# Two transformer blocks: the first norm's factor moves from the input of the first two loads to their drains, and the first load comes in two halves

## The reference, cut to what matters

```
def rms_norm(x, g):
    y = x * rsqrt(mean(x * x, axis=-1, keepdims=True) + EPS)
    return y * g

h = rms_norm(x, norm_mix_g)
proj = h @ w_in                              # [256, 7 * 1024]
sc_b, sc_c, sc_x, cf_a, cf_g, gate_sc, gate_cf = split(proj)
cf = (cf_a + cf_b_pw1[:1024]) * sigmoid(cf_g + cf_b_pw1[1024:])
```

## Time and profile before

| | |
|---|---|
| median of three executions | 1431.58 us (1431.01 to 1433.02) |
| profiled execution, its time | 1430.79 us |
| its span (first to last instruction) | 1428.7 us |
| TensorE busy | 1309.6 us, 92% |
| DVE, ACT, POOL busy | 945.6, 498.5, 452.0 us |
| mean granted clock of TensorE | 0.971 |
| first matmul of the first load | 11.55 us |
| first matmul of a split load | 27.40 us |

### The profile page before, as it was taken

One profiled execution on the slowest core, in us unless ns is written; L12 is line 12 of the kernel. 1 busy time (PEld: TensorE's weight loads), 2 busy tenths in 40 slices (PEclk: granted clock), 3 DMA queues, 4 the chain that ended last, 5 costly groups with the idle time before them and its releaser, 6 DMA issues.

```text
span 1428.7 us, 25109 instructions
## 1 busy us (share of the span) xinstructions
PE 1309.6 (92%) x9622; PEld 1233.8 (86%) x9622; DVE 945.6 (66%) x2085; ACT 498.5 (35%) x973; POOL 452.0 (32%) x326
## 2 busy tenths in 40 slices
PE   9999999999999987886888787888899999999998
PEld 8999999998888986886878786878886789989997
DVE  4689987675594775859586767755525546666665
ACT  5533456445223121211202221211225445553443
POOL 1588822000133654453635453564203000000000
PEclk9999999999999999898989999999999999999999
DMA  7555554552599999999999999999862023465552
GB/s 280 195 190 189 178 177 165 190 177 92 215 424 353 419 426 428 427 428 427 428 426 426 427 425 428 426 428 427 352 255 83 29 90 133 149 203 181 177 185 81
DMA packets 57895, 397.91 MB, mean 279 GB/s; under 512 B 6352, under 2 KB 9040, under 8 KB 10192
## 3 DMA queue, kind: packets, MB, share of 16 engines
q0 software_dynamic: 36864, 268.45, 44.9%
q1 hardware_dynamic: 20944, 128.28, 25.3%
HBM read 395.66 MB, written 1.05 MB: 278 GB/s over the span
## 4 chain that ended last, share of the span: by engine, by line
PE 57%; DMA 20%; DVE 12%; issue 6%; ACT 3%; POOL 1%; DVEq 0%; POOLq 0%; ACTq 0%
DMA rows_late<-peer_uv_dram,stage 20%; PE bank L765 11%; PE bank L767 11%; PE bank L766 11%; PE bank L1023 7%; PE bank L728 6%; PE bank L749 4%; DVE rows_late L2105 4%; ACT w_hi L1259 1%; PE bank L889 1%; POOL rows_late L665 1%; DVE probs L2029 1%; DVE probs L2031 1%; DVE pick L2032 1%; DVE w_lo L548 1%
## 5 line engine op out<-in xcount | busy, mean ns | idle before, releaser
L1023 PE MATMUL bank<-diag,rows_late 128*128 128x128 f32 x2816 | 325.1, 277 | 26.3 <-ACT diag L1452 26.3
L1023 PEld LDWEIGHTS bank<-diag,rows_late 128*128 128x128 f32 x2816 | 321.3, 194 | 29.2 <-ACT diag L1452 29.1
L2105 DVE SCALAR_TENSOR_TENSOR rows_late<-rows_late,squares 128x1024 f32<-128x1024 f32 x176 | 213.1, 1228 | 127.1 <-DMA rows_late<-peer_uv_dram,stage 111.0
L1023 PE MATMUL bank<-diag,rows_early 128*128 128x128 f32 x1280 | 172.7, 302 | 75.4 <-ACT diag L1452 75.4
L1023 PEld LDWEIGHTS bank<-diag,rows_early 128*128 128x128 f32 x1280 | 167.2, 215 | 81.4 <-ACT diag L1452 80.9
L665 POOL DMA_INDIRECT rows_late<-peer_uv_dram,stage x165 | 192.8, 1169 | 136.9 <-PE bank L1023 95.0
L1259 ACT ACTIVATE w_hi<-raw 128x2048 fp32r<-128x2048 f32 x94 | 179.3, 1909 | 118.2 <-PE bank L767 109.9
L765 PE MATMUL bank<-x_hi_a,w_hi 128*128 128x256 f32 x672 | 190.9, 284 | 2.7 <-DVE x_lo_a L1672 1.8
L766 PE MATMUL bank<-x_lo_a,w_hi 128*128 128x256 f32 x672 | 190.2, 283 | 0.0
L767 PE MATMUL bank<-x_hi_a,w_lo 128*128 128x256 f32 x672 | 190.1, 283 | 0.0
L548 DVE TENSOR_TENSOR w_lo<-raw,w_hi 128x2048 fp32r<-128x2048 f32 x66 | 151.2, 2292 | 49.9 <-ACT w_hi L1259 45.2
(11 more groups left out here) (357 smaller groups left out, 1877.3 us busy)
## 6 DMA issues: line engine op xcount, KB each, us to landing
raw<-w_in_dram SPq DMA_DIRECT2D x28, 1024.0 KB, 5.0
raw<-w_up_dram SPq DMA_DIRECT2D x16, 1024.0 KB, 5.0
raw<-w_down_dram SPq DMA_DIRECT2D x16, 1024.0 KB, 4.9
rows_late<-w_in_dram SPq DMA_DIRECT2D x10, 1024.0 KB, 8.5
raw<-w_kv_dram SPq DMA_DIRECT2D x8, 1024.0 KB, 4.8
rows_late<-w_peer_q_dram SPq DMA_DIRECT2D x5, 1024.0 KB, 12.2
raw<-sc_w_out_dram SPq DMA_DIRECT2D x4, 1024.0 KB, 4.8
raw<-cf_w_pw_dram SPq DMA_DIRECT2D x4, 1024.0 KB, 4.8
```

The lines of the kernel that those rows point to most:

```text
L1023: mm = nc.tensor.matmul(ct(Y_ACC[c][t // 4], t % 4, P), expert_rows(k)[:, D + t * P:D + (t + 1) * P], ct(diag, k % DIAGS, P), start=False, ...
L2105: w_.scalar_tensor_tensor(out=row, in0=row, scalar=1.0, in1=h_tok[:, c * D:(c + 1) * D], op0=ALU.mult, op1=ALU.mult, accum_out=pre[:, side ...
```

## The change

Before its matmuls of the first two loads TensorE no longer waits for the norm's factor. DVE multiplies x by the norm's weights alone into a free buffer (gate_cf) as soon as vec and x are there, and the plain matmuls read that. The factor is the same for a whole column of an output tile, so it enters at the drains. The statistics run behind the fifth input tile of load 0, the spread behind the seventh; the fillers between them are gone, and two more stand in the opening. DVE copies the spread factor to SBUF (rstd), makes h_norm from gate_cf and rstd for the later loads, and drains g0 and g1 to SBUF times rstd; ACT's sigmoid then works in place there. For a0 and a1 DVE first multiplies the bank by rstd into a small buffer (turns) and then does the former instruction on that. ACT's rounding of load 2 now stands in front of its roundings of h. SP issues load 0 in two halves right behind vec, ahead of the identity, and load 2 ahead of the other constants.

```
--- before.py
+++ after.py
@@ -98,7 +98,7 @@
         p.append((None, 0, [(name, first + i) for i in range(n)], engine))
 
     for b in range(4):
-        add("w_in", [16 + b], "g", 2, "act", 2 * b)
+        add("w_in", [16 + b], "g", 2, "act" if b else "dve", 2 * b)
         add("w_in", [12 + b], "a", 2, "dve", 2 * b)
     for b in range(4):
         add("w_in", [4 + b], "c", 2, "act", 2 * b)
@@ -594,11 +597,13 @@
                 sp.dma_start(whole(i), T[name][b]).then_inc(whole_landed[at], 16)
 
             sp.dma_start(vec[:], T["vecs"]).then_inc(vec_landed, 16)
+            name, b = LOADS[0]
+            sp.dma_start(ring(raw, 0)[:, 0:SLOT // 2], T[name][b][:, 0:SLOT // 2]).then_inc(first_half_landed, 16)
+            sp.dma_start(ring(raw, 0)[:, SLOT // 2:], T[name][b][:, SLOT // 2:]).then_inc(raw_landed[0], 16)
             sp.dma_start(ident, T["consts"][:, 0:P]).then_inc(ident_landed, 16)
-            load(0)
             load(1)
+            load(2)
             sp.dma_start(const[:, P:], T["consts"][:, P:]).then_inc(const_landed, 16)
-            load(2)
             sp.dma_start(mem_raw.rearrange("p (t s) -> p t s", t=DT),
                          T["mem_t"].rearrange("(t p) s -> p t s", p=P)).then_inc(mem_landed, 16)
             sp.dma_start(pos_i, T["positions_2"].to_broadcast([P, SEQ])).then_inc(pos_landed, 16)
@@ -737,16 +742,22 @@
                     pe.wait_ge(query_landed[n - RING], 16)
                 else:
                     w = ring(raw, i)
-                    pe.wait_ge(raw_landed[i % RING], 16 * RAW_COUNT[i])
+                    if i:
+                        pe.wait_ge(raw_landed[i % RING], 16 * RAW_COUNT[i])
+                    else:
+                        pe.wait_ge(first_half_landed, 16)
                 outs = [open_tile(name, n) for n in which]
+                x_gain = h_norm if norm_name == "peer" else gate_cf
                 for k in range(DT):
+                    if i == 0 and k == DT // 2:
+                        pe.wait_ge(raw_landed[0], 16)
                     if norm_name == "peer":
                         pe.wait_ge(peer_scaled, k + 1)
                     else:
-                        pe.wait_ge(normed, NORMED[norm_name] - DT + k + 1)
+                        pe.wait_ge(x_gained, k + 1)
                     for j, out in enumerate(outs):
                         at = k * 256 + j * P
-                        mm = nc.tensor.matmul(out[:, 0:SEQ], w[:, at:at + P], ct(h_norm, k),
+                        mm = nc.tensor.matmul(out[:, 0:SEQ], w[:, at:at + P], ct(x_gain, k),
                                               start=(k == 0), stop=(k == DT - 1))
                         if k == DT - 1:
                             mm.then_inc(acc_ready, 1)
@@ -915,22 +926,26 @@
                                  start=False, stop=True).then_inc(acc_ready, 1)
 
             pe.wait_ge(filled, 2)
-            keep_busy(10)
+            keep_busy(12)
             pe.wait_ge(filled, 4)
-            for j in range(DT // 2):
-                pe.wait_ge(summed, j + 1)
-                for c in range(NC):
-                    mm = nc.tensor.matmul(STAT[:, c:c + 1], ct(squares, 2 * j)[:, c * P:(c + 1) * P], mean_d[:, 0:1],
-                                          start=(j == c == 0), stop=(j == DT // 2 - 1 and c == NC - 1))
-                if j == DT // 2 - 1:
+
+            def first_norm(k):
+
+                if k == 4:
+                    for j in range(DT // 2):
+                        pe.wait_ge(summed, j + 1)
+                        for c in range(NC):
+                            mm = nc.tensor.matmul(STAT[:, c:c + 1], ct(squares, 2 * j)[:, c * P:(c + 1) * P],
+                                                  mean_d[:, 0:1], start=(j == c == 0),
+                                                  stop=(j == DT // 2 - 1 and c == NC - 1))
                     mm.then_inc(stat_ready, 1)
-                keep_busy(1 if j < DT // 2 - 1 else 2)
-            pe.wait_ge(ident_landed, 16)
-            spread("mix")
-            keep_busy(1)
+                elif k == 6:
+                    pe.wait_ge(ident_landed, 16)
+                    spread("mix")
+
             for b in range(4):
                 if b == 0:
-                    linear_plain("g", range(2), LOAD_OF["g", 0], "mix")
+                    linear_plain("g", range(2), LOAD_OF["g", 0], "mix", first_norm)
                     linear_plain("a", range(2), LOAD_OF["a", 0], "mix")
                 else:
                     linear("g", range(2 * b, 2 * b + 2), "w_in", 16 + b, "h1", DT, 256)
@@ -1340,10 +1355,16 @@
             square("mix", lambda k: act.wait_ge(x_landed[k // 4], 16), x_res)
             act.wait_ge(filled, 6)
             root("mix")
+            round_to(2)
             split_all("h1", normed_tile("mix"), h_norm)
             for b in range(4):
                 for i in range(2 * b, 2 * b + 2):
-                    drain("g", i, ct(sig, i), ACT.Sigmoid, bias=v("cf_b_pw1", 8 + i))
+                    if b:
+                        drain("g", i, ct(sig, i), ACT.Sigmoid, bias=v("cf_b_pw1", 8 + i))
+                    else:
+                        ahead("g", i)
+                        wait_drained(act, "g", i)
+                        s.activation(ct(sig, i), ct(sig, i), ACT.Sigmoid, bias=v("cf_b_pw1", 8 + i)).then_inc(first_sig, 1)
                 ahead("a", 2 * b)
                 if b == 0:
                     act.wait_ge(mem_landed, 16)
@@ -1697,21 +1718,40 @@
             def freed(ins):
                 return done(ins, acc_freed["dve"])
 
-            for j in range(DT // 2):
-                dve.wait_ge(squared, square_count("mix", 2 * j + 1))
-                w_.tensor_tensor(ct(squares, 2 * j), ct(squares, 2 * j), ct(squares, 2 * j + 1), ALU.add).then_inc(summed, 1)
             dve.wait_ge(vec_landed, 16)
-            norm("mix", x_res, "norm_mix_g", h_norm)
+            for half in range(2):
+                dve.wait_ge(x_landed[half], 16)
+                for k in range(4 * half, 4 * half + 4):
+                    w_.tensor_scalar(ct(gate_cf, k), ct(x_res, k), v("norm_mix_g", k), None, ALU.mult).then_inc(x_gained, 1)
+                for j in range(2 * half, 2 * half + 2):
+                    dve.wait_ge(squared, square_count("mix", 2 * j + 1))
+                    w_.tensor_tensor(ct(squares, 2 * j), ct(squares, 2 * j), ct(squares, 2 * j + 1), ALU.add).then_inc(summed, 1)
+            dve.wait_ge(x_gained, DT)
+            link(w_.tensor_copy(rstd[:], rstd_of("mix")))
+            for k in range(DT):
+                tok = done(w_.tensor_tensor(ct(h_norm, k), ct(gate_cf, k), rstd[:], ALU.mult), normed)
+            dve.wait_ge(*tok)
             split_all("h1", h_norm)
+            for i in range(2):
+                wait_tile(dve, "g", i)
+                freed(w_.tensor_tensor(ct(sig, i), acc("g", i), rstd[:], ALU.mult))
 
             dve.wait_ge(filled, 4)
             for i in range(8):
                 ahead("a", i)
                 wait_tile(dve, "a", i)
-                wait_drained(dve, "g", i)
-                tok = freed(w_.scalar_tensor_tensor(out=ct(cf_in, i, CFW)[:, CFK - 1:], in0=acc("a", i),
-                                                    scalar=v("cf_b_pw1", i), in1=ct(sig, i),
-                                                    op0=ALU.add, op1=ALU.mult))
+                if i < 2:
+                    dve.wait_ge(*freed(w_.tensor_tensor(turns[:], acc("a", i), rstd[:], ALU.mult)))
+                    dve.wait_ge(first_sig, i + 1)
+                    tok = done(w_.scalar_tensor_tensor(out=ct(cf_in, i, CFW)[:, CFK - 1:], in0=turns[:],
+                                                       scalar=v("cf_b_pw1", i), in1=ct(sig, i),
+                                                       op0=ALU.add, op1=ALU.mult), dve_step)
+                    dve.wait_ge(*tok)
+                else:
+                    wait_drained(dve, "g", i)
+                    tok = freed(w_.scalar_tensor_tensor(out=ct(cf_in, i, CFW)[:, CFK - 1:], in0=acc("a", i),
+                                                        scalar=v("cf_b_pw1", i), in1=ct(sig, i),
+                                                        op0=ALU.add, op1=ALU.mult))
                 if i == 1:
                     for k in range(DT):
                         add_to_sum("mem", k)
```

More of the change, by code:

```diff
@@ L447, in two_blocks @@
         vec_landed = sem("vec_landed")
+        first_half_landed = sem("first_half_landed")
+        x_gained = sem("x_gained")
+        first_sig = sem("first_sig")
         ident_landed = sem("ident_landed")
```

## The result

The changed kernel took 1438.99 us (median of 6 runs, 1437.93 to 1440.37) against 1432.12 for the kernel before (6 runs, 1431.01 to 1433.63): ratio 1.0047, 95% interval 1.0037 to 1.0057. That is 6.9 us slower, where 0.9 us faster was forecast. So the two profiles are 9.6 us apart where the medians are 6.9 apart.

A forecast was written before the change was run, and what follows sets the result against it. TensorE, busy for 92% of the span, was taken as the bound. Split matmuls 1.1 us earlier plus 0.2 us of new wait gave -0.9 us, from 1431.58 to 1430.7 us; range 1428.8 to 1432.6.

The forecast's parts named there:

- The start: Opening: load matmuls wait only for the first gained tile and half load, so start at 8.3, 3.25 us earlier.
- Statistics and spread among the matmuls: Opening on TensorE: statistics groups add about 1.7 us, the spread 0.5; root and reciprocal are hidden behind tiles 5 and 6.
- The clock in the opening: Under the load matmuls: 1.2 GHz from 9.1 to 12.6, costing 1.75 us; first split matmul at 26.3, 1.1 us earlier.
- The drains: DVE's chain after the spread: products 2.77 us, mem sums 3.59, w_lo of load 4 ready at 38.25; g's banks cause no wait.
- The wait for w_lo of load 4: TensorE before load 4's split matmuls: wants w_lo at 38.24, waits between 0 and 0.9 us, taken as 0.2.
- so it moves along: Later stretch bound by the expert rows' DMA: begins when TensorE's scores are known, so it shifts with TensorE; no term given.
- a gain at 50 us is not there any more at the end: Sign of being wrong: a lead won in the opening has vanished by the kernel's end.
- R3: DVE's chain takes over: the wait for w_lo of load 4 is 0.9 to 1.1 us, total 1431.5; chance 0.12.
- R1: Opening: the clock doesn't fall, split matmuls start from 24.6, total 1429.0 us; chance 0.17.
- R2: Opening: the clock falls and stays low as long as before, costing 3.4 us, total 1432.2; chance 0.16.
- R4: Opening: the half load lands no sooner than the whole (9.6), total 1432.3 us; chance 0.05.
- The range: Total time from 1428.8 to 1432.6 us, reaching from R1 to R2 with half a microsecond of scatter.

The follow-up runs named there:

- f1_probe: The kernel before with one more POOL subtract of w_lo's form on unused data, started beside DVE's eight products and first x_lo: 1429.88 us (one run).
- c1_all: Changed kernel with the products' factor read from PSUM, POOL's w_lo of load 5 after the mem sums, and ACT rounding load 2 before the root: 1431.69 us.
- a2_no_reorder: c1_all with ACT's root ahead of its rounding of load 2 again, leaving only the two edits against DVE-POOL collisions: 1431.41 us, ratio 0.9996.
- c4_root_first: c1_all with eight more fillers ahead of the first load matmul and ACT's root before its rounding of load 2 again: 1430.23 us, ratio 0.9986.
- b1_sums_first: Changed kernel with POOL's w_lo of load 5 started only when DVE's sums for mem are done: 1435.62 us, ratio 1.0029.

## Why the prediction was wrong, point by point

- **The start: right.** 8.24 for 8.3. The half load landed at 8.15. The first gained tile takes 0.35 us and is there at 7.3. The second half landed at 9.43, 1.3 us behind the first, so the fixed 2.0 us that the prediction quotes from the Trainium skill isn't added between these queued transfers, as the identity's row had said. (The section quoted describes transfers that GpSimd issues; these are SyncE's.)
- **Statistics and spread among the matmuls: right.** 1.7 and 0.44 us (14.32 to 16.02, 17.83 to 18.27) for 1.7 and 0.5, and the root and reciprocal hidden behind tiles 5 and 6.
- **The clock in the opening: right in its price, in part by luck.** It was down from 8.2 to 11.65, where 9.1 to 12.6 was forecast. Both ends came 0.9 early, and the fillers ended at 5.8, not 6.7; only the length, 3.4 for 3.5 us, was right. Two later falls were not forecast. And the 1.1 us of gain came from a profile in which the clock was down for 6.8 us; f1_probe, with the same opening, was down for 3.4, and two profiles of the changed opening not at all. One profile of each could not give this term.
- **The drains: the step that failed.** It said "eight products at the pace of eight x_lo (2.77)" and put the sums for "mem" at 3.59. The products took 6.61 us and the sums 7.81, because one instruction of each stood still for the rest of a POOL instruction. I had taken durations from stretches in which POOL was idle and had not asked what POOL does at the new time. The text even names the cause, that ACT's w_hi of load 2 stands earlier and POOL's w_lo follows it, but it asks only whether that ends in time (before 23; it ended at 22.92), not what it runs beside. POOL's w_lo of load 5, the other partner, stands nowhere in the sum. So the term for new waits of TensorE, 0.2 us, measured 5.6 (2.6 for the drain of g, 1.6 for the sums, 1.4 for w_lo), and two low stretches of the clock came behind the waits. The Trainium skill, "SBUF — State Buffer", section "Who interferes with whom", has the rule: a DVE instruction with two SBUF inputs contends with a GpSimd instruction that reads SBUF, and the one that starts second is blocked in full. The runs agree: 4264 and 4632 ns where 410 and 425 are usual, 476 ns unchanged with the second operand in PSUM, and POOL's 6.62 for 4.6 us when DVE was first. With it the rows alone give up to 4.5 us, POOL's own duration, for each of the two places.
- **The wait for w_lo of load 4, taken as 0.2: about right once nothing on DVE collides.** c1_all had 0.19 us to spare by the trace; a2_no_reorder and c4_root_first, with the clock high all along and the first x_lo held, waited 0.6.
- **"so it moves along", of the expert layer: not borne out.** The prediction gave the expert layer no term, since its start moves with TensorE. Its start does move, but its end doesn't by the same amount (table above): c4_root_first goes in with a lead of 2.4 us and comes out with 0.4. That "a gain at 50 us is not there any more at the end" was one of the prediction's own signs of being wrong.
- **The rivals.** R3 named the right place (w_lo of load 4 is late) for the wrong reason, and with a third of its price. R1 came true in the profiles of a2_no_reorder and b1_sums_first. R2 and R4 did not occur in a profile.
- **The range.** It held all cases of the clock and none of a collision, though the change gives DVE eight instructions whose second operand is newly in SBUF, just where a POOL instruction had come close behind before (16.95 to 17.69).

What stays open: the mechanism of the two long instructions and of TensorE's waits is shown, and so is that the two edits against them take the whole excess away. How the 6.9 us of the medians divide is not: the shares of the single collisions don't add up, the expert layer adds up to 3.8 us in the profiles for a reason that no run isolates, and the share of the clock differs from execution to execution.

## What to carry to other kernels

When an edit moves an elementwise instruction or changes where its second operand lies, look up what the other engine of the pair runs at its new time, not only what its inputs wait for. Leaving one operand in PSUM, where it already was, kept DVE's products clear of POOL, and an instruction far longer than its group's median is the sign in a profile, since it counts as busy. And before a difference of a microsecond is forecast from one profile, ask which of its terms (here the clock in the opening) differ between executions of the same program, and whether the lead is still there behind the last stage that something else bounds (here the expert layer).

## What the runs showed of the hardware that I had not expected

- DVE and POOL hold each other up for the rest of an instruction in both orders. Behind POOL, single DVE instructions went from 0.41 to 4.26 us, from 0.43 to 4.63, and from 0.41 to 1.26 where less of POOL's instruction was left. Behind DVE's w_lo, POOL went from 4.6 to 6.62, and behind its x_lo_b, in the kernel before, to 5.59.
- A product with one operand in PSUM is no slower than with both in SBUF: eight take 2.73 against 2.77 us for eight x_lo.
- The same opening on TensorE ran with 3.4 us or with 6.8 us at 1.2 GHz (f1_probe and the profile before), which moved everything up to 341 us by 1.7 us.
